# One-core Strassen-Winograd projection kernel: first token tile multiplied before its norm, and DMA loads and stores issued in smaller parts at other steps

## What is computed

```python
h = rms_norm(x, pre_norm)                   # per token over 1024
proj = h @ w_in                             # 1024 -> 3*1024 + 1536 + 512
p, gate, mq = split(proj)
b_gate, c_gate, u = split(p, 3)
mix = b_gate * conv3(c_gate * u)            # causal, 3 taps
kv = rms_norm(mem, mem_norm) @ w_mem_kv     # 256 memory rows
mem_o = softmax(mq @ k.T * 128**-0.5) @ v   # 4 heads of 128
y = (concat(mix, mem_o) * silu(gate)) @ w_out
out = x + rms_norm(y, post_norm)
```

## Time and profile before

| | |
|---|---|
| median of 3 runs | 2178.57 us |
| profiled execution, whole | 2178.16 us |
| its span, first to last instruction | 2176.3 us |
| TensorE busy | 2152.8 us (99%) |
| VectorE / ScalarE / GpSimd busy | 1209.7 / 745.6 / 174.7 us |
| DMA moved | 550 MB, 253 GB/s on average |
| granted TensorE clock, mean | 0.999 |

### The profile page before, as it was taken

The page is one execution under the profiler, slowest core; times in us unless marked ns, Lnnn a source line. Parts: engine busy times, 40 slices in busy tenths (PEclk is TensorE's granted clock), DMA queues, the critical chain, the costliest instruction groups (busy, mean ns, idle before and its releaser), DMA issues.

```text
span 2176.3 us, 26536 instructions
## 1 busy us (share of the span) xinstructions
PE 2152.8 (99%) x9820; PEld 1782.1 (82%) x9820; DVE 1209.7 (56%) x1819; ACT 745.6 (34%) x1312; POOL 174.7 (8%) x285
## 2 busy tenths in 40 slices
PE   8999999999999999999999999999999999999998
PEld 7888888888888888788887888888887788888887
DVE  7668767643335353354345237576764755566665
ACT  5444333411221342221123233545351633333333
POOL 0000000000000000111100000101010111111110
PEclk9999999999999999999999999999999999999999
DMA  6897777678766778987877765656667866666665
GB/s 242 306 339 277 274 268 269 244 252 274 243 217 217 267 263 307 335 287 265 295 233 257 247 226 190 223 193 218 198 204 291 337 252 240 238 232 227 247 228 193
DMA packets 157103, 550.33 MB, mean 253 GB/s; under 512 B 18032, under 2 KB 18064, under 8 KB 153904
## 3 DMA queue, kind: packets, MB, share of 16 engines
q1 hardware_dynamic: 122048, 416.34, 54.9%
q0 software_dynamic: 34928, 132.30, 17.3%
HBM read 404.90 MB, written 143.67 MB: 252 GB/s over the span
## 4 chain that ended last, share of the span: by engine, by line
PE 89%; DMA 4%; DVE 4%; ACT 1%; issue 1%; SPq 0%; DVEq 0%; ACTq 0%
PE banks L1701 29%; PE banks L1703 29%; PE banks L1702 29%; DMA slots<-w_split 3%; PE banks L1818 1%; DVE hop_lo L1307 1%; DVE x_in L1275 1%; ACT hop_hi L983 1%; ACT probs L1074 0%; DMA mw_stream<-mw_kept 0%; DMA raws<-in_w_in 0%; DMA raws<-in_w_kv 0%; DVE rmax L1483 0%; DVE pt_lo L1498 0%; DVE mix L1467 0%
## 5 line engine op out<-in xcount | busy, mean ns | idle before, releaser
L1701 PE MATMUL banks<-hop_hi,slots 128*128 128x512 f32 x2184 | 853.1, 391 | 8.3 <-DMA slots<-w_split 8.0
L1702 PE MATMUL banks<-hop_lo,slots 128*128 128x512 f32 x2184 | 850.4, 389 | 0.0
L1703 PE MATMUL banks<-hop_hi,slots 128*128 128x512 f32 x2184 | 850.0, 389 | 0.0
L1701 PEld LDWEIGHTS banks<-hop_hi,slots 128*128 128x128 f32 x2184 | 410.1, 188 | 97.3 <-DMA slots<-w_split 13.2
L1703 PEld LDWEIGHTS banks<-hop_hi,slots 128*128 128x128 f32 x2184 | 409.9, 188 | 86.1
L1702 PEld LDWEIGHTS banks<-hop_lo,slots 128*128 128x128 f32 x2184 | 410.1, 188 | 83.1
L1703 PE MATMUL banks<-hop_hi,out_slot 128*128 128x512 f32 x448 | 175.4, 392 | 0.0
L1701 PE MATMUL banks<-hop_hi,out_slot 128*128 128x512 f32 x448 | 175.3, 391 | 0.0
L1702 PE MATMUL banks<-hop_lo,out_slot 128*128 128x512 f32 x448 | 175.2, 391 | 0.0
L1357 DVE TENSOR_TENSOR out_slot<-out_raws,out_slot 128x768 fp32r<-128x768 f32 x112 | 107.3, 958 | 90.3 <-ACT out_slot L937 90.3
L1414 DVE TENSOR_TENSOR u<-banks,u 128x512 f32<-128x512 f32 x54 | 37.3, 691 | 210.5 <-PE banks L1703 210.5
(11 more groups left out here) (188 smaller groups left out, 2602.1 us busy)
## 6 DMA issues: line engine op xcount, KB each, us to landing
slots<-w_split SPq DMA_DIRECT2D x406, 512.0 KB, 4.2
w_split<-slots SPq DMA_DIRECT2D x140, 512.0 KB, 3.5
mw_stream<-mw_kept SPq DMA_DIRECT2D x96, 512.0 KB, 4.5
out_raws<-g_kept POOLq DMA_DIRECT2D x60, 384.0 KB, 6.1
raws<-in_w_in SPq DMA_DIRECT2D x86, 256.0 KB, 4.5
x_in<-in_x_t SPq DMA_DIRECT2D x16, 1024.0 KB, 8.2
g_kept<-mix POOLq DMA_DIRECT2D x32, 512.0 KB, 6.9
x_res<-in_x POOLq DMA_DIRECT2D x32, 512.0 KB, 5.3
```

What stands on the lines that cost most here:

```text
L1701: nc.tensor.matmul(dst, a, c, start=first, stop=False, skip_group_check=True)
L1702: nc.tensor.matmul(dst, a, d, start=False, stop=False, skip_group_check=True)
L1703: return nc.tensor.matmul(dst, b, c, start=False, stop=last, skip_group_check=True)
```

## The change

Five things.

1. Start. TensorE multiplies the raw x of tile 0, with only the gain put in (`raw_hi`, `raw_lo`), and the first outputs of tile 0 are multiplied by the tokens' factor afterwards (`first_scale`, VectorE). x comes first on SP's queue, in pieces of 256 KB, and the rows for the squares later. The second warm-up is gone. Tile 1 is normed first, tile 0's norm (`norm(0, k)`) comes after. The last operand's difference, split and low part (`last_sum`, `last_hi`, `last_lo`) move behind steps R5, R6 and R7 of pair 2. The counter `hop_lo_done` therefore reaches its full value for macro-tile 0 only with `last_lo(1)`.
2. x for the next macro-tile comes in 16 parts of 256 KB at steps 16, 20, ..., 76 (`X_QUARTERS`). The first, at step 16 of macro-tile 0, waits for that full value.
3. q, m and g results are stored block by block (256 KB), one step at a time (`keep_block`); so are the output sums.
4. In macro-tile 3 `mem` comes in four parts at now = 7 to 10, the first two key/value blocks at now = 11 and 13 instead of 6 and 9, and block b from 2 on at now = KV_AT[b-2] + 1 instead of KV_AT[b-2].
5. Before the output phase the loads of 1 MB and the four blocks stand further apart (`OUT_X_AT`, `OUT_BLOCKS_AT`), and `memory_rows_in(0)` comes 9 to 13 steps earlier.

The core of the diff:

```diff
-WARM = (26, 14)
+WARM = 26
-X_AFTER = {2: 0, 3: 2, 4: 1, 5: 3}
+X_QUARTERS = {16 + 4 * q: ((0, 2, 1, 3)[q // HK], q % HK) for q in range(4 * HK)}
-OUT_X_AT = [122, 123, 124, 125]
+OUT_X_AT = [122, 124, 127, 131]
+OUT_BLOCKS_AT = [126, 129, 133, 135]
+ROWS_AT = [127, 131]
+MEM_AT = (7, 8, 9, 10)
+def hop_all(m):
+    return m * PRODUCTS - PRODUCTS + len(FIRST_OPERANDS)
@@ SP, macro-tile 0
             for p, r in ORDER[:UNITS0]:
                 keep_unit(p, r)
                 if r == R1 and p < PAIRS - 1:
                     load_raw(p + 1, X11)
                     load_raw(p + 1, X21)
                 if r == R3 and p < PAIRS - 1:
                     load_raw(p + 1, X22)
                     load_raw(p + 1, X12)
-                if r == R4 and p in X_AFTER:
-                    sp.wait_ge(hop_lo_done, PRODUCTS)
-                    load_x(X_AFTER[p], 1)
+                if PRODUCTS * p + r in X_QUARTERS:
+                    sp.wait_ge(hop_lo_done, hop_all(1))
+                    load_x_quarter(*X_QUARTERS[PRODUCTS * p + r], 1)
@@ SP, macro-tile 3
-                        if now == 2:
-                            sp.wait_ge(hop_lo_done, (m + 1) * PRODUCTS)
-                            sp.dma_start(mem_in[:], mem).then_inc(mem_dma, 16)
+                        if now in MEM_AT:
+                            sp.wait_ge(hop_lo_done, hop_all(m + 1))
+                            two = slice(2 * MEM_AT.index(now), 2 * MEM_AT.index(now) + 2)
+                            sp.dma_start(mem_in[:, two, :], mem[:, two, :]).then_inc(mem_dma, 16)
-                        if now in (6, 9):
-                            load_kv((now - 6) // 3)
+                        if now in (11, 13):
+                            load_kv((now - 11) // 2)
-                        if now in KV_AT and KV_AT.index(now) + 2 < KV_BLOCKS:
-                            load_kv(KV_AT.index(now) + 2)
+                        if now - 1 in KV_AT and KV_AT.index(now - 1) + 2 < KV_BLOCKS:
+                            load_kv(KV_AT.index(now - 1) + 2)
@@ GpSimd's queue
+            def keep_block(p, r):
...
+                    pool.dma_start(q_kept[m, 2 * (i - FIRST_Q) + f, t], zb[:, n, HALO:]).then_inc(q_kept_dma, 16)
...
+            def keep(p, r):
+                if p >= DIRECT and kind_of(p) in "qm" and r in (R3, R7, R2, R4):
+                    keep_block(p, r)
+                if kind_of(p) == "g" and r in (R7, R2, R4):
+                    keep_block(p, {R7: R3, R2: R7, R4: R2}[r])
+                if p and kind_of(p - 1) == "g" and r == R1:
+                    keep_block(p - 1, R4)
@@ VectorE, start: after the first halves
+            token_sum(0, 0)
...
+            first_scale(0)
             operand_lo(0, R5)
+            first_scale(2)
             token_sum(0, 1)
+            norm(0, 4)
+            norm(0, 5)
             token_sum(0, 2)
             operand_lo(0, R6)
+            norm(0, 6)
+            norm(0, 7)
             operand_lo(0, R7)
@@ VectorE, pair 2
+                    if p == DIRECT and r == R1:
+                        operand_lo(0, R2)
+                    if p == DIRECT and r == R7:
+                        last_lo(0)
+                        last_lo(1)
+                        ahead(m, step - 1)
+                    if p != DIRECT or r != R3:
+                        ahead(m, step)
+                    if p == DIRECT and r == R5:
+                        last_sum(0)
+                        last_sum(1)
@@ TensorE
-            warm(WARM[0])
-            spread(0)
-            warm(WARM[1])
-            multiply_first(0)
...
+            warm(WARM)
+            for n in range(len(FIRST)):
                 multiply_first(n)
+                    if (n, k) == (5, 2):
+                        spread(1)
+                    elif (n, k) == (9, 0):
+                        spread(0)
```

More of the change, by code:

```diff
@@ new lines, in raw_hi, with half_hi @@
+            def raw_hi(k):
+                act.wait_ge(first_x_dma[piece_of(k)], 16)
+                nc.scalar.activation(hop_hi[:, (R1, R2)[k // HK], k % HK, :], x_in[:, 0, k, :], ACT.Copy,
+                                     scale=gains[:, 0, k:k + 1]).then_inc(first_hop_hi, 1)
+            def half_hi(r, half, y, done):
+                two = slice(2 * half, 2 * half + 2)
+                act.wait_ge(normed, done + 2 * half + 2)
+                if r == R1:
+                    act.wait_ge(first_done, 4)
+                nc.scalar.activation(hop_hi[:, r, two, :], y[:, two, :], ACT.Copy).then_inc(first_hop_hi, 1)
@@ L1119, in _ @@
             nc.scalar.activation(ysd[:, 0:1], eps[:], ACT.Sqrt)
-            for c in range(SUB):
-                square(0, c)
-            root(0)
-            first_units_hi(X11)
-            for half in range(2):
-                two = slice(2 * half, 2 * half + 2)
-                act.wait_ge(normed, 2 * half + 2)
-                nc.scalar.activation(hop_hi[:, R1, two, :], Y11[:, two, :], ACT.Copy).then_inc(first_hop_hi, 1)
-            first_units_hi(X21)
+            first_unit_halves(0, X11)
@@ L1129, in _ @@
+            act.wait_ge(small_dma, 32)
+            for k in range(HK):
+                raw_hi(k)
+            first_unit_halves(1, X11)
+            first_unit_halves(0, X21)
+            first_unit_halves(1, X21)
+            raw_hi(4)
+            raw_hi(5)
+            first_unit_halves(0, X12)
+            unit_hi(DIRECT, R1)
+            unit_hi(DIRECT, R5)
+            raw_hi(6)
+            raw_hi(7)
+            first_unit_halves(1, X12)
+            unit_hi(DIRECT, R6)
             for c in range(SUB):
@@ L1557, in _ @@
-            for half in range(2):
-                two = slice(2 * half, 2 * half + 2)
-                dve.wait_ge(first_hop_hi, half + 1)
-                nc.vector.tensor_tensor(hop_lo[:, R1, two, :], Y11[:, two, :], hop_hi[:, R1, two, :].bitcast(f32),
-                                        ALU.subtract).then_inc(first_hop_lo, 1)
-            first_units_lo(X21)
-            dve.wait_ge(x_dma[2], 16)
-            for k in range(HK, KT):
-                norm(0, k)
-            inverse(1)
-            first_units_lo(X12)
@@ new lines, in raw_lo, with half_lo @@
+            def raw_lo(k):
+                at_k = (slice(None), (R1, R2)[k // HK], k % HK, slice(None))
+                dve.wait_ge(first_hop_hi, k + 1)
+                nc.vector.scalar_tensor_tensor(out=hop_lo[at_k], in0=x_in[:, 0, k, :], scalar=gains[:, 0, k:k + 1],
+                                               in1=hop_hi[at_k].bitcast(f32), op0=ALU.mult, op1=ALU.subtract).then_inc(first_hop_lo, 1)
+            def half_lo(r, half, y, done):
+                two = slice(2 * half, 2 * half + 2)
+                dve.wait_ge(first_hop_hi, done + half + 1)
+                nc.vector.tensor_tensor(hop_lo[:, r, two, :], y[:, two, :], hop_hi[:, r, two, :].bitcast(f32),
+                                        ALU.subtract).then_inc(first_hop_lo, 1)
@@ new lines, in _ @@
+            first_unit_rest(0, X11)
+            for k in range(HK):
+                raw_lo(k)
+            first_unit_rest(1, X11)
+            first_unit_rest(0, X21)
+            first_unit_rest(1, X21)
+            raw_lo(4)
+            raw_lo(5)
+            first_unit_rest(0, X12)
+            weight_sum(DIRECT, R5)
+            split_lo(UNIT_OF[DIRECT, R1], unit_source(DIRECT, R1))
+            weight_sum(DIRECT, R6)
+            raw_lo(6)
+            raw_lo(7)
+            first_unit_rest(1, X12)
@@ new lines, in _ @@
+            split_lo(UNIT_OF[DIRECT, R5], unit_source(DIRECT, R5))
+            split_lo(UNIT_OF[DIRECT, R6], unit_source(DIRECT, R6))
+            first_inverse(1)
+            first_unit_rest(0, X22)
+            first_unit_rest(1, X22)
+            norm(1, 0)
+            norm(1, 1)
+            weight_sum(DIRECT, R3)
+            weight_sum(DIRECT, R7)
+            norm(1, 2)
+            norm(1, 3)
+            half_lo(R6, 0, Y12, KT)
+            half_lo(R6, 1, Y12, KT)
+            first_inverse(0)
@@ L1771, in multiply @@
                 for k in tiles:
+                    if p == DIRECT and r == R4 and k == 2:
+                        pe.wait_ge(hop_lo_done, hop_count(m, r))
                     w = [a[:, k * P:(k + 1) * P] for a in unit(u)]
```

433 lines of the change are left out of this document (261 added, 172 removed).

## The result

After the change the kernel takes 2206.72 us in the median of four runs (2201.29 to 2209.37), against 2178.25 before on the same chip. The ratio is 1.012, with a 95% interval of 1.010 to 1.014. The kernel is slower by 28.5 us, where the forecast of 2188.5 stood 10.3 above the profiled execution of before, and 2206.72 lies above the range. The profiled execution took 2209.37 us, its span 2207.6.

What follows compares the result with a forecast made beforehand. TensorE, busy 99%, was taken to bound the kernel. From 2178.2 us: start -0.2, slots -9.4, streamed rows -0.5, old block 6 wait -1.1, key/value waits +21.5, giving 2188.5; range 2184 to 2195, or 2183 to 2198 with rivals and bounds.

Steps and rivals of the forecast that it cites:

- both places of loss: New waits of TensorE: some 4.5 us at pair 3, and six of 3.59 us in the key/value stretch.
- both chains: Pair 3 waits for SP's queue, held until `last_lo(1)`; key/value products wait for blocks fetched behind the next slot load.
- The start: Up to pair 3: first product at 11.1 us, pair 2 5.6 us earlier, but only 0.2 us saved at pair 3.
- the wait that takes the saving back: TensorE at pair 3 waits some 4.5 us for loads queued behind SP's wait, giving back 4.9 us.
- The key/value waits: Blocks 2 to 7 arrive late, TensorE waits six times 3.59 us: 21.5 us, bounds 19 to 25.
- L - 0.91: TensorE's wait per late key/value block: 0.37 + L + 1.44 - 2.72 us.
- L: Landing time of a key/value block from its issue, taken as 4.5 us; 3.2 by the skill page.
- The clock: Rival: each of six key/value gaps drops TensorE to 1.2 GHz, 1.7 us a fall, 10 in all, 2198.5; chance 0.12.
- The slots: All nine TensorE waits for weight slots go with the smaller DMAs: 9.4 us saved, bounds 4 to 9.4.
- after the change each step adds 256 to 512 KB: Beside a slot load's 512 KB, so at most 1 MB moves per step of 2.72 us.
- rival 2: Smaller DMAs do not free the weight slots, only 4 us of the 9.4 come back: 2194; chance 0.10.
- The streamed rows: TensorE's wait for streamed memory rows, beside g's last store, shrinks by 0.5 us, from 0 to 1.1.

Runs made afterwards that it cites:

- e3: Kernel of e1 with 15 small matmuls, written to an unread bank, ahead of each of the six late key/value products: 2203.3 us, ratio 1.011.
- e1: Kernel before with one change, key/value blocks 2 to 7 fetched one step later: 2210.5 us, ratio 1.015.
- e2: Changed kernel with key/value blocks 2 to 7 fetched at their old step again: 2175.7 us, ratio 0.998.
- e4: Changed kernel with the sixteen parts of x issued from step 20 instead of 16: 2199.7 us, ratio 1.010.
- e8: Changed kernel, key/value fetch at its old step, x from step 20, each half of a `w_conv` sum on GpSimd's queue held to its step: 2171.7 us, ratio 0.994.
- e6: Kernel of e8 with key/value blocks 2 to 7 fetched one step ahead of their old place: 2164.3 us, ratio 0.992.
- e7: Kernel before with x of the next macro-tile in 16 parts of 256 KB from step 20, instead of four of 1 MB: 2177.8 us, ratio 0.999.
- e9: Kernel of e1 with 5 small matmuls ahead of each late key/value product, where e3 has 15: 2212.3 us, ratio 1.015.

## Why the prediction was right and wrong

The direction, both places of loss and both chains were right. The sum against the profiled execution was +10.3; measured is +31.2. By its steps:

1. **The start, forecast -0.2, measured +3.4.** The first product (11.1, measured 11.4), the end of `last_lo(1)` (74.6, measured 74.7) and the wait that takes the saving back were right. Two things were not. The raw block took 5.5 us where I used the 4.5 of the earlier trace rows: the same kind of block behind the same kind of store, but now with a quarter of x ahead of both, which I priced with its issue of 0.4 us and no bytes. That its bytes made the 1 us is likely and not tested. And the wait of 5.9 us cost the clock: 3.4 - 1.5 = 1.9 us more.
2. **The key/value waits, forecast 6 x 3.6 = 21.5, measured 23.6.** The formula L - 0.91 holds to 0.3 us: with L = 4.6 it gives 3.7, measured 3.9 in the mean. Of the 2.1 us, L makes 0.8 and the constant, nearer 0.7, the rest. The prediction's estimate of 3.2 for L rests on a fit that the Trainium skill, "DMA: Bandwidth & Descriptors", section "Anatomy of one DMA", gives for the path of GpSimd's DMAs, while these blocks go out on SP's queue; the six took 4.5 to 4.9.
3. **The clock: the step that failed.** I had the right price (1.7 us a fall; 1.6 to 1.75 by three pairs of runs, and 1.5 by e3) from the clock's first microseconds, and put it into a rival with a chance of 0.12, because the wait of 2.1 us in before had not done it. That row spoke for waits of 2.1 and not for 3.6, and I let the nearest row below decide. It was also one case of something that goes both ways: the same wait, in the same code, lost the clock in e3 (last section). For the long waits there was no exception: the clock fell behind all 20 of 3.2 us and more in after, e1, e2 and e4, seven of them in after, for about 12 us. With this term alone the forecast would have been 2198.5 plus the fall at pair 3, 2200. The Trainium skill, "TensorE: Matmul & The Clock Gate", was named there with the rule that an idle TensorE is put back to 1.2 GHz; the trace agrees for the seven waits of 3.6 to 5.9 us, and for waits near 2 us only in some cases.
4. **The slots, forecast -9.4.** All nine old waits went, as forecast, but four new ones lost 4.2 us, so 5.2 came back. The failed step is "after the change each step adds 256 to 512 KB": true of SP, whose queue is released step by step, and not of GpSimd's, which waits only for its data and runs on when that comes. The gate of e8 and e6 bears this out in direction; its size is open. The mild form of rival 2 (only 4 us come back) met the size, by another mechanism.
5. **The streamed rows, forecast -0.5.** There is one wait of 1.6 us where there was one of 0.9, so +0.7. I ran no experiment on it.

Together: 3.6 for the start, 10.5 for the clock and 2.1 for the longer waits in the key/value stretch, and 5 to 6 for slots and streamed rows make up the 20.9 us between forecast and measurement, to within 1.

## What to carry to other kernels

Price a new wait of the bounding engine twice: its length, and what the clock costs behind it; here each of TensorE's waits of 3.2 us and more, and some of those near 2, cost some 1.4 to 1.9 us more, and the busy share hides it, so look at the clock column and at matmuls counted per microsecond. When a load is moved one step later, compare its landing with the slack from issue to use, not with its bandwidth: here the slack was 2.7 us of TensorE's work and the landing 4.6. And cutting DMAs smaller spaced them out on the queue that is released step by step; on the one that waits for data alone pieces of two steps left together.

## What had not been expected of the hardware

The length of a wait does not alone decide whether the clock falls. In before TensorE waited 2.1 us at 15.5 and kept 2.4 GHz; busy by stretch, right behind it:

```profile
17.60:20.60 3.00, 3.00 (x13) 2.48 (x14) 3.00 (x5) 3.00 (x7) 0.00 (x0) 1.00 1.02 406
20.60:23.60 3.00, 3.00 (x15) 2.48 (x14) 2.50 (x7) 2.80 (x6) 0.00 (x0) 1.00 1.04 408
```

In e3, where nothing is changed before the key/value stretch, the same matmul waited just as long, and there the clock fell: 8 matmuls in 3.3 us, and pair 2 starts 1.7 us later than in before (63.8 against 62.1). TensorE's wait, and busy by stretch behind it:

```profile
PE banks L1701 <- DVE hop_lo L1560: 2.1, 1, 2.1
17.70:21.00 3.30, 3.30 (x8) 2.63 (x9) 3.30 (x5) 3.30 (x7) 0.00 (x0) 0.51 1.01 401
21.20:24.50 3.30, 3.30 (x16) 2.71 (x15) 2.79 (x9) 2.87 (x8) 0.00 (x0) 1.00 1.03 407
```

So the same program can go either way from one execution to the next. That is why e3 and e7 reach pair 3 at 86 us in the table of the experiments and before at 84.6. Over the eleven traces, with the idle times as the profile prints them: all 20 waits of 3.2 us and more lost the clock (six each in after, e1 and e4, and those at pair 3 in after and e2), and none up to 1.7 us did. Of the 19 from 1.9 to 3.0 us, 11 lost it, among them five of the six in e9, and 8 did not, the longest of these 2.6 us in e7. The first wait of each execution, before any matmul, is left out. What distinguishes these 19 stays open.
